# Layer 1 of a five-layer network on Trainium2: modulation by halves, merging products by parts in their own banks, the next norm's transposes taken from X, and GpSimd's bias work later

## The chip, the cores and the metric

The kernel runs on one NeuronCore of one Trainium2 chip. The metric is the device time of one execution in microseconds (us), the median of three runs. "The profile" is that of one further execution; its times count from the first instruction. Engines: PE is TensorE (matrix products), PEld its weight loads, DVE is VectorE, ACT is ScalarE, POOL is GpSimd, SP is SyncE, which issues most transfers here.

## The reference, cut to what matters

Three blocks follow one another on 256 tokens of width 1024; the change touches the first block and the seam to the second.

```python
# block 1
mod = c @ w_ada + b_ada;  shift, scl, gate = split(mod, 3)
h = rms_norm(x, g_norm) * (1 + scl) + shift
u, z_pool, q, k, v, z_attn, m_pool, m_attn = split(h @ w_in, ...)      # 5120 columns
y_pool = (pooling(u) * silu(z_pool)) @ w_pool_up                       # 512 -> 1024
y_attn = (attention(rope(q), rope(k), v) * silu(z_attn)) @ w_attn_up   # 512 -> 1024
merged = sigmoid(m_pool) * y_pool + sigmoid(m_attn) * y_attn
x = x + gate * (merged @ w_out)
x = rms_norm(x, g_final)
# block 2 begins
h = rms_norm(x, ev_attn_norm);  proj = h @ ev_w_in                     # 3072 columns
```

## The kernel before, in words

All weights pass through one stream of chunks of 128x2048 float32 (1 MB), numbered in the order of their use. SP loads chunk n into `ring` (6 slots; it waits until the chunk 6 before it has been split), ACT copies it to `WH` rounded to float32r ("hi", L951), DVE subtracts to give `WL` ("lo", L955); both have 3 slots, so hi of chunk n waits until PE has consumed chunk n-3. PE then makes each product as three: WH with XTH, WL with XTH, WH with XTL (`three`, L400 to L402), where XTH and XTL are the transposed activations, split alike. A full chunk is 24 such instructions. Chunks 0 to 3 are the scale columns of w_ada, 4 to 7 the shift columns, 8 to 27 w_in (`P1`), 28 to 31 the gate columns of w_ada, 32 and 33 w_pool_up (`UP1`), 34 and 35 w_attn_up (`AUP1`), 36 to 39 w_out (`OUT1`), 40 to 51 ev_w_in (`P2`).

The order on every engine is written out by hand, one program per engine; engines meet at semaphores only. `split_until(eng, n)` makes ACT or DVE split all chunks below n at that place of its program, so whatever stands behind it waits for these splits; `used(eng, n)` waits until PE has consumed chunk n. `Transposes` (names beginning with T) lets PE transpose 128x128 tiles (L306) into banks 4 to 7, two tiles per step i; ACT writes XTH (L314), DVE XTL (L327).

Stages in order around the change:

- Modulation (`ada_products`, L2116): the condition vector times w_ada gives rows of 2x512, which are copied to SBUF by `ADA_ROWS` (L1390 on ACT, L1611 on DVE) and turned into columns by tiny products (`ada_columns`, L2125). From these come SCALE and SHIFT (L1616 to L1621), with which ACT makes XTH (L1395) and DVE XT1 and XTL (L1626, L1629) out of the transposed, normed input (`T1`).
- `P1`, heads, pooling and attention `A1`.
- `TY1`, gate products, `TA1`, a product that spreads the gate to all partitions (L2177, banks 6 and 7), `UP1` and `AUP1` into banks 0 to 3, DVE's products with the sigmoids (L1669) after each, one sum (L1672), transposes `TM1`, `OUT1`.
- `OUT1` closes by parts (`PARTS`: half of the columns, tile of tokens): for each part DVE multiplies by the gate (L1685), adds to X (L1686) and multiplies by g_final into O (L1688). `T2` transposes O, `P2` follows. The two norms are merged into one scale per token (`stat`, L1696 to L1702), computed beside P2; POOL then writes the normed X (L1270), which `P2`'s work on DVE waits for at its second job.
- POOL turns the relative-position biases (four transfers issued by ACT at L1420) into the form that a later layer adds (L1264, L1266).

## Time and profile before

| what | value |
|---|---|
| median of 3 runs | 2199.08 us (2198.71 to 2203.82) |
| profiled execution, its own time | 2200.07 us |
| its span, first to last instruction | 2198.3 us |
| PE busy / DVE busy / ACT busy / POOL busy | 92% / 71% / 60% / 5% |
| chain that ended last, by engine | PE 81%, DVE 9%, ACT 6%, issue 3% |
| mean granted TensorE clock | 0.961 of 2.4 GHz |

A clock of 0.5 is 1.2 GHz. Busy shares are means over stages with different limits; the stages in question lie in the first 300 us of the span.

### The profile page before, as it was taken

How to read it: one execution, taken by the hardware profiler on the slowest of the kernel's cores; microseconds unless marked ns; L12 is line 12 of the kernel's file. 1: busy time of each engine (PE TensorE's matmuls, PEld its weight loads, DVE VectorE, ACT ScalarE, POOL GpSimd, SP SyncE). 2: the span in 40 equal slices, each digit the busy share in tenths (PEclk: the TensorE clock that was granted, in tenths of full speed). 3: DMA queues.
4: the chain of work that ended last, by engine and by line, in shares of the span. 5: the costliest groups of instructions: out<-in, count | busy, mean ns of one | idle time of the engine just before them, and what ended most of it. 6: DMA issues, size and time to landing. Idle time of an engine off the chain costs nothing.

```text
span 2198.3 us, 26390 instructions
## 1 busy us (share of the span) xinstructions
PE 2033.0 (92%) x9736; PEld 1674.3 (76%) x9736; DVE 1550.9 (71%) x1719; ACT 1310.8 (60%) x1395; POOL 120.4 (5%) x101
## 2 busy tenths in 40 slices
PE   5998797799999989999999999999999999999687
PEld 2885686678887878787888878787877877787576
DVE  5546673554458678888888888888889854664565
ACT  5445267344444467777777777777776755444243
POOL 0000210000000042000000000000006001000000
PEclk8999899899999999999999999999999999999688
DMA  9554541455545159999999999999999956144100
GB/s 350 170 175 162 155 174 59 154 171 186 195 158 189 58 222 395 364 392 356 389 362 373 384 363 385 358 383 354 391 360 380 348 172 229 53 162 137 39 1 29
DMA packets 233215, 535.16 MB, mean 243 GB/s; under 512 B 12457, under 2 KB 23733, under 8 KB 233142
## 3 DMA queue, kind: packets, MB, share of 16 engines
q1 hardware_dynamic: 222464, 515.80, 65.3%
q10 hardware_dynamic: 8854, 12.07, 1.6%
q0 software_dynamic: 1824, 6.31, 0.8%
q8 instruction: 47, 0.77, 0.1%
q14 instruction: 26, 0.21, 0.0%
HBM read 521.02 MB, written 13.12 MB: 243 GB/s over the span
## 4 chain that ended last, share of the span: by engine, by line
PE 81%; DVE 9%; ACT 6%; issue 3%; DMA 0%; ACTq 0%; DVEq 0%; POOLq 0%; POOL 0%
PE bank L400 23%; PE bank L402 23%; PE bank L401 23%; DVE WL L955 3%; PE bank L514 3%; ACT WH L951 3%; PE bank L526 1%; PE bank L306 1%; PE bank L2341 1%; PE bank L540 1%; PE bank L538 1%; PE bank L536 1%; PE bank L367 1%; ACT XTH L1115 1%; DMA X<-in_x 0%
## 5 line engine op out<-in xcount | busy, mean ns | idle before, releaser
L955 DVE TENSOR_TENSOR WL<-ring,WH 128x2048 fp32r<-128x2048 f32 (+1 forms) x487 | 1118.0, 2308 | 360.4 <-ACT WH L951 358.1
L951 ACT ACTIVATE WH<-ring 128x2048 fp32r<-128x2048 f32 (+1 forms) x487 | 927.8, 1910 | 415.6 <-PE bank L402 404.8
L400 PE MATMUL bank<-WH,XTH 128*128 128x512 f32 (+2 forms) x1936 | 761.0, 393 | 31.0 <-DVE WL L955 7.3
L401 PE MATMUL bank<-WL,XTH 128*128 128x512 f32 (+2 forms) x1936 | 750.6, 388 | 0.0
L402 PE MATMUL bank<-WH,XTL 128*128 128x512 f32 (+2 forms) x1936 | 750.0, 387 | 0.0
L400 PEld LDWEIGHTS bank<-WH,XTH 128*128 128x128 f32 x1936 | 369.6, 191 | 112.3 <-issue 25.1
L402 PEld LDWEIGHTS bank<-WH,XTL 128*128 128x128 f32 x1936 | 369.1, 191 | 74.7
L401 PEld LDWEIGHTS bank<-WL,XTH 128*128 128x128 f32 x1936 | 369.9, 191 | 70.5
L400 PE MATMUL bank<-WH,HTH 128*128 128x512 f32 x540 | 212.7, 394 | 11.3 <-DVE HTL L1915 5.5
L402 PE MATMUL bank<-WH,HTL 128*128 128x512 f32 x540 | 210.2, 389 | 0.0
L401 PE MATMUL bank<-WL,HTH 128*128 128x512 f32 x540 | 209.9, 389 | 0.0
L400 PEld LDWEIGHTS bank<-WH,HTH 128*128 128x128 f32 x540 | 101.4, 188 | 36.5 <-DVE WL L955 14.8
L402 PEld LDWEIGHTS bank<-WH,HTL 128*128 128x128 f32 x540 | 101.5, 188 | 21.3
L401 PEld LDWEIGHTS bank<-WL,HTH 128*128 128x128 f32 x540 | 101.6, 188 | 20.2
L551 ACT ACTIVATE scr<-scr,nmax 128x128 f32<-128x128 f32 (+1 forms) x160 | 71.4, 447 | 71.3 <-DVE nmax L565 71.0
L437 ACT ACTIVATE P<-bank,stat 128x512 f32<-128x512 f32 (+1 forms) x56 | 34.7, 671 | 90.1 <-PE bank L402 90.1
L1529 ACT ACTIVATE P<-bank 128x512 f32<-128x512 f32 x56 | 33.5, 598 | 40.3 <-PE bank L402 40.3
L1333 POOL DMA_INDIRECT P<-rows,P x4 | 6.8, 1701 | 808.4 <-POOLq L1328 807.4
L514 PE MATMUL bank<-KT,QT 128*128 128x256 f32 (+1 forms) x176 | 43.0, 369 | 7.7 <-ACT P L437 2.5
L565 DVE CUSTOM_DVE_ANT_0 scr<-bank,UNSEEN 128x128 f32<-128x128 f32 x96 | 30.4, 355 | 27.2 <-PE bank L514 26.4
L575 DVE COPY scr<-bank 128x384 f32<-128x384 f32 x80 | 44.2, 553 | 3.9 <-PE bank L526 3.9
L1010 ACT ACTIVATE P<-X 128x1024 f32<-128x1024 f32 x14 | 15.1, 1075 | 43.2 <-DVE X L1040 33.7
(405 smaller groups left out, 1553.5 us busy)
## 6 DMA issues: line engine op xcount, KB each, us to landing
ring<-in_od_we_gate SPq DMA_DIRECT2D x112, 1024.0 KB, 6.7
ring<-in_od_we_up SPq DMA_DIRECT2D x112, 1024.0 KB, 7.0
ring<-in_od_we_down SPq DMA_DIRECT2D x112, 1024.0 KB, 6.6
ring<-in_w_in SPq DMA_DIRECT2D x20, 1024.0 KB, 5.2
ring<-in_fox_w_in SPq DMA_DIRECT2D x16, 1024.0 KB, 5.3
ring<-in_nsa_w_in SPq DMA_DIRECT2D x14, 1024.0 KB, 5.0
ring<-in_w_ada SPq DMA_DIRECT2D x12, 1024.0 KB, 8.6
ring<-in_ev_w_in SPq DMA_DIRECT2D x12, 1024.0 KB, 5.1
```

What stands on the lines that cost most here:

```text
L306: last = nc.tensor.transpose(bank[4 + i % 4][:, j * S + tt * 128:j * S + tt * 128 + 128], src(tt), ident[:, :])
L400: nc.tensor.matmul(out, x[0], wt[0][:, k, :], start=start, stop=False, skip_group_check=check)
L401: nc.tensor.matmul(out, x[0], wt[1][:, k, :], start=False, stop=False, skip_group_check=check)
L402: return nc.tensor.matmul(out, x[1], wt[0][:, k, :], start=False, stop=stop, skip_group_check=check)
L437: last = nc.scalar.activation(dest(tt), bank[(2 * c + tt) % 4][:, 0:width], func, scale=stat[:, self.scale + tt:self.scale + tt + 1] if se ...
L514: last = nc.tensor.matmul(b[:, a:a + n], q[:, a:a + 128], k[:, 128 - 128 * t0:256], start=True, stop=not self.pe_mask, skip_group_check=True)
L551: last = nc.scalar.activation(e, e, ACT.Exp, bias=nmax[:, i % 3, t0:t0 + 1], scale=-1.0, accum_out=rs[:, g % 2, t0, uu:uu + 1])
L565: last = nc.vector.tensor_tensor_reduce(out=E[i % 3][:, a:a + n], in0=bank[4 + i % 2][:, a:a + n], in1=self.bias(i, t0), scale=1.0, scalar ...
L575: nc.vector.tensor_copy(PT[j % 2], bank[6 + j % 2][:, 0:384]).then_inc(copied, 1)
L951: nc.scalar.activation(wh, slot_ap(n, nk, width), ACT.Copy).then_inc(hi_made, 1)
L955: nc.vector.tensor_tensor(wl, slot_ap(n, nk, width), wh.bitcast(F32), ALU.subtract).then_inc(lo_made, 1)
L1529: nc.scalar.activation(MHID[:, f % 2, 0, :], bank[f % 2 * 2][:, :], ACT.Silu).then_inc(m_silu, 1)
```

## The change: what it does

1. **Input.** X is loaded by SP ahead of chunk 0, where ACT loaded it beside the ring. The late rows of `vec` (b_ada, g_norm and now g_final) are transposed by PE after chunk 0 in a step of their own; DVE copies them and multiplies g_final by ev_attn there.
2. **Modulation.** The shift columns are read as two halves of 512 columns over all of the depth (chunks 4, 5 and 6, 7), each in its own bank. Each half is turned into columns, and X's columns of that half are made, apart from the other. ACT copies all rows and writes XT1 for even steps. ACT and DVE split chunks 8 and 9 between the halves, where they were split ahead of SHIFT.
3. **Merging.** PE goes from `TA1` straight to `UP1`; `AUP1` writes banks 4 to 7, so it does not wait for DVE. Both close by parts, and DVE multiplies and adds part by part. The spreading of the gate comes after `AUP1`, in banks 0 and 1. `TM1` starts when half of the columns is merged.
4. **Seam.** `T2` transposes X with the scale g_final times ev_attn. DVE's four products with g_final move behind `T2` as two of 128x1024, and the last split of `OUT1` (chunk 41) moves behind these. ACT squares X after `T2`.
5. **POOL** scales X first and works on the biases after it.

```diff
@@ -204,7 +204,8 @@
-        c_scale, c_shift = ada_chunks(1), ada_chunks(0)
+        c_scale = ada_chunks(1)
+        c_shift = [cols(w["w_ada"], 512 * i, 512) for i in range(2)]
@@ -654,18 +656,20 @@
-        UP1 = OutProduct(c_pup, xt)
-        up_used = sem("up_used")
+        up_used, up_ps = sem("up_used"), sem("up_ps")
+        UP1 = OutProduct(c_pup, xt, part_ps=up_ps)
...
-        AUP1 = OutProduct(c_aup, lambda kt, tt: xt(4 + kt, tt))
+        AUP1 = OutProduct(c_aup, lambda kt, tt: xt(4 + kt, tt), lambda half, tt: bank[4 + 2 * half + tt], up_ps)
@@ -708,7 +712,7 @@
-        T2 = Transposes(normed(("ev_attn", 0)), split=True)
+        T2 = Transposes(normed(("g_final", 0), X), split=True)
@@ -1181,6 +1185,8 @@
+            for tt in range(TT):
+                sp.dma_start(X[:, tt, :], t["x"].rearrange("b (t p) n -> p (b t) n", p=128)[:, tt, :]).then_inc(ada_in, 16)
             for n in range(N0):
                 load(n)
@@ -1384,17 +1388,28 @@
-            for i, chunks in enumerate((c_scale, c_shift)):
-                split_until(act, chunks[-1][0] + SPLIT)
-                used(act, chunks[-1][0])
-                nc.scalar.activation(ADA_ROWS[i][:, 0:512], bank[2 * i][0:2, :], ACT.Copy).then_inc(ada_rows, 1)
-            act.wait_ge(ada_set, 2)
-            for i in range(T1.n):
+            split_until(act, c_shift[1][0][0] + 1)
+            used(act, c_scale[-1][0])
+            for h in range(2):
+                nc.scalar.activation(ADA_ROWS[0][:, 512 * h:512 * h + 512], bank[h][0:2, :], ACT.Copy).then_inc(ada_rows, 1)
+            split_until(act, c_shift[1][1][0] + 1)
+
+            def x_columns(i):
                 act.wait_ge(turn_ready, T1.b + i + 1)
-                for k in range(2 * i, 2 * i + 2):
-                    last = nc.scalar.activation(XTH[:, k, :], bank[4 + i][:, k % 2 * S:k % 2 * S + S], ACT.Identity,
-                                                bias=SHIFT[:, k:k + 1], scale=SCALE[:, k:k + 1])
+                for dest in (XTH, XT1) if i % 2 == 0 else (XTH,):
+                    for k in range(2 * i, 2 * i + 2):
+                        out = XTH[:, k, :] if dest is XTH else XT1[:, k // 4, k % 4, :]
+                        last = nc.scalar.activation(out, bank[4 + i][:, k % 2 * S:k % 2 * S + S], ACT.Identity,
+                                                    bias=SHIFT[:, k:k + 1], scale=SCALE[:, k:k + 1])
                 last.then_inc(turn_act, 1)
+
+            for h in range(2):
+                used(act, c_shift[h][-1][0])
+                nc.scalar.activation(ADA_ROWS[1][:, 512 * h:512 * h + 512], bank[2 + h][0:2, :], ACT.Copy).then_inc(ada_rows, 1)
+                act.wait_ge(ada_set, 2 + h)
+                for i in range(2 * h, 2 * h + 2):
+                    x_columns(i)
+                split_until(act, c_in1[0][0][0] + 1 + h)
@@ -1420,13 +1435,11 @@
             OUT1.splits(act)
-            act.wait_ge(x_half, 3)
-            square(act, 0, X)
             T2.act(act)
-            act.wait_ge(x_half, 4)
-            square(act, 1, X)
-            for tt in range(TT):
-                act.wait_ge(y_half, 3 + tt)
+            for tt in range(TT):
+                square(act, tt, X)
+            for tt in range(TT):
+                act.wait_ge(y_half, 1 + tt)
@@ -1655,25 +1669,27 @@
-            split_until(dve, c_gate1[-1][0] + SPLIT)
+            split_until(dve, c_gate1[-1][0] + SPLIT - 1)
+            TA1.dve(dve)
             used(dve, c_gate1[-1][0])
             nc.vector.tensor_copy(GATE_ROWS[0:2, 512:1024], bank[7][0:2, :]).then_inc(gate_rows, 1)
-            TA1.dve(dve)
...
+            for s, (stage, c0) in enumerate(((UP1, 3072), (AUP1, 4096))):
                 stage.splits(dve)
...
+                for i, (half, tt) in enumerate(PARTS):
+                    if i < 3:
+                        dve.wait_ge(up_ps, 3 * s + i + 1)
+                    else:
+                        stage.wait(dve)
+                    m = P[:, tt, c0 + half * 512:c0 + half * 512 + 512]
+                    nc.vector.tensor_tensor(m, stage.outs(half, tt)[:, :], m, ALU.mult).then_inc(up_used, 1)
+                    if s:
+                        dve.wait_ge(up_used, 4 + i + 1)
+                        both_ = P[:, tt, 3072 + half * 512:3584 + half * 512]
+                        nc.vector.tensor_tensor(both_, both_, m, ALU.add).then_inc(merged, 1)
@@ -1684,11 +1700,12 @@
-                dve.wait_ge(x_half, i + 1)
-                nc.vector.tensor_tensor(O[:, tt, at_h], X[:, tt, at_h], GAIN[:, at_h], ALU.mult).then_inc(y_half, 1)
-                if i == 0:
-                    OUT1.splits(dve)
             T2.dve(dve)
+            dve.wait_ge(gfin_in, 16)
+            dve.wait_ge(x_half, 4)
+            for tt in range(TT):
+                nc.vector.tensor_tensor(O[:, tt, :], X[:, tt, :], GAIN, ALU.mult).then_inc(y_half, 1)
+            OUT1.splits(dve)
@@ -2119,21 +2137,26 @@
-            def ada_columns(i):
-                pe.wait_ge(ada_rows, 2 * i + 2)
-                for k in range(KD):
...
+            def ada_columns(row, k0, n, out, count):
+                pe.wait_ge(ada_rows, count)
+                for k in range(n):
...
             ada_products(c_scale[2:], bank[0:2])
-            ada_products(c_shift[0:1], bank[2:4])
-            ada_columns(0)
-            ada_products(c_shift[1:], bank[2:4])
-            ada_columns(1)
+            ada_products(c_shift[0], bank[2:3])
+            ada_columns(0, 0, 8, bank[0], 2)
+            ada_products(c_shift[1][0:1], bank[3:4])
+            ada_columns(1, 0, 4, bank[2], 3)
+            ada_products(c_shift[1][1:], bank[3:4])
+            ada_columns(1, 4, 4, bank[3], 4)
@@ -2172,22 +2195,21 @@
             TA1.pe(pe)
+            UP1.pe(pe, closes=True)
+            TA1.wait(pe)
             pe.wait_ge(gate_rows, 2)
+            AUP1.pe(pe, closes=True)
+            pe.wait_ge(up_used, 4)
             for half_ in range(2):
-                last = nc.tensor.matmul(bank[6 + half_][:, :], ones[0:3, :], GATE_ROWS[0:3, 512 * half_:512 * half_ + 512],
+                last = nc.tensor.matmul(bank[half_][:, :], ones[0:3, :], GATE_ROWS[0:3, 512 * half_:512 * half_ + 512],
                                         start=True, stop=True)
             last.then_inc(gate_ps, 1)
-            UP1.pe(pe)
-            TA1.wait(pe)
-            pe.wait_ge(up_used, 1)
-            AUP1.pe(pe)
-            pe.wait_ge(merged, 1)
+            TM1.pe(pe, lambda i: pe.wait_ge(merged, 2 if i < 2 else 4))
             pe.wait_ge(gate_set, 2)
-            TM1.pe(pe)
             OUT1.pe(pe, operand=TM1, closes=True)
 
 
-            T2.pe(pe, lambda i: pe.wait_ge(y_half, 2 if i < 2 else 4))
+            T2.pe(pe, halves_ready(pe, 0))
```

DVE's queue in the modulation, from the split behind the scale's row on (WL<-ring is a split, the stat rows are SCALE and SHIFT, P<-bank is XT1). Before:

```order
L1618 TENSOR_TENSOR stat<-stat,vec 128x8 [waits dve_chain]
L955 TENSOR_TENSOR WL<-ring,WH 128x2048 [waits hi_made] x4
L1611 COPY P<-bank 2x512 [waits consumed]
L1621 TENSOR_TENSOR stat<-bank,vec 128x8 [waits ada_cols]
L1626 TENSOR_SCALAR P<-bank,stat 128x256 [waits turn_act,ada_set]
```

Of the change:

```order
L1628 TENSOR_TENSOR stat<-stat,vec 128x8 [waits dve_chain]
L959 TENSOR_TENSOR WL<-ring,WH 128x2048 [waits hi_made]
L1632 TENSOR_TENSOR stat<-bank,vec 128x4 [waits ada_cols]
L1642 TENSOR_TENSOR XTL<-P,XTH 128x512 [waits turn_act,ada_set]
L1639 TENSOR_SCALAR P<-bank,stat 128x256 [waits turn_act]
L1639 TENSOR_SCALAR P<-bank,stat 128x256
L1642 TENSOR_TENSOR XTL<-P,XTH 128x512 [waits dve_chain]
L959 TENSOR_TENSOR WL<-ring,WH 128x2048 [waits hi_made]
L1632 TENSOR_TENSOR stat<-bank,vec 128x4 [waits ada_cols]
```

Four splits stood between SCALE and SHIFT; now one does, then half of SHIFT and of X's columns, and the next split follows that.

DVE's queue at the seam, from OUT1's first part on (O<-bank is the gate's product, QT holds the gate, KT g_final, XTL<-bank is T2). Before:

```order
L1685 TENSOR_TENSOR O<-bank,QT 128x512 [waits norm_out_ps,gate_set]
L1686 TENSOR_TENSOR X<-X,O 128x512 [waits dve_chain]
L1688 TENSOR_TENSOR O<-X,KT 128x512 [waits norm_half]
L955 TENSOR_TENSOR WL<-ring,WH 128x2048 [waits hi_made]
L1685 TENSOR_TENSOR O<-bank,QT 128x512 [waits norm_out_ps]
```

Of the change, the last part and what follows it:

```order
L1701 TENSOR_TENSOR O<-bank,QT 128x512 [waits consumed]
L1702 TENSOR_TENSOR X<-X,O 128x512 [waits dve_chain]
L328 SCALAR_TENSOR_TENSOR XTL<-bank,vec,XTH 128x256 [waits turn_act]
...
L1707 TENSOR_TENSOR O<-X,KT 128x1024 [waits norm_half,gfin_in]
L1707 TENSOR_TENSOR O<-X,KT 128x1024
L959 TENSOR_TENSOR WL<-ring,WH 128x2048 [waits hi_made]
```

The split of chunk 41 stood behind the first part and ahead of the other three; it is now the last of all.

POOL's queue around the scaling of X (P<-UNSEEN,P and P<-P are the biases). Before:

```order
L1264 TENSOR_TENSOR P<-UNSEEN,P 128x8x128 [waits rel_in,mask_set]
L1266 TENSOR_SCALAR P<-P 128x8x128
L1264 TENSOR_TENSOR P<-UNSEEN,P 128x8x128
L1266 TENSOR_SCALAR P<-P 128x8x128
L1270 TENSOR_SCALAR X<-O,stat 128x1024 [waits ms_ready,rel_set]
L1270 TENSOR_SCALAR X<-O,stat 128x1024
```

Of the change:

```order
L1269 TENSOR_SCALAR X<-O,stat 128x1024 [waits ms_ready,mask_set]
L1269 TENSOR_SCALAR X<-O,stat 128x1024
L1274 TENSOR_TENSOR P<-UNSEEN,P 128x8x128 [waits rel_in,norm_done]
L1276 TENSOR_SCALAR P<-P 128x8x128
```

The two scalings changed places with the four operations on the biases.

## Rows read from the trace of the kernel before

**Rows 1.** The page: the span.

```profile
span 2198.3 us, 26390 instructions
```

**Rows 2.** The chain that ended last, to P1's first product: start, us, what.

```profile
2.58 10.25 DMA X<-in_x
...
18.45 2.30 DVE WL L955
20.79 3.53 PE bank L2116 x8
...
45.50 3.58 PE bank L2125 x16
...
51.47 0.70 DVE XTL L1629
...
52.31 0.77 PE bank L400
```

**Rows 3.** Timeline of ACT in the modulation: start, us, engine, line, instructions.

```profile
7.88 1.89 ACT L951 ACTIVATE WH<-ring 128x2048 fp32r<-128x2048 f32 x1
...
49.77 3.29 ACT L1395 ACTIVATE XTH<-bank,stat 128x256 fp32r<-128x256 f32 x7
```

**Rows 4.** Windows: chunk 8, UP1, AUP1, OUT1; the number behind POOL is the clock.

```profile
52.30:60.90 8.60, 8.59 (x26) 6.88 (x27) 6.86 (x10) 2.57 (x4) 0.00 (x0) 0.65 0.22 55
203.80:216.70 12.90, 12.82 (x49) 10.06 (x48) 4.63 (x3) 4.80 (x4) 0.00 (x0) 0.87 0.68 219
219.40:233.50 14.10, 14.02 (x48) 10.96 (x48) 4.28 (x3) 1.92 (x1) 0.00 (x0) 0.78 0.29 93
241.60:264.20 22.60, 22.50 (x98) 18.31 (x96) 13.96 (x12) 8.46 (x7) 10.51 (x3) 0.98 0.77 233
```

**Rows 5.** Timeline of PE and DVE from TA1 to TM1.

```profile
198.75 1.04 PE L306 MATMUL bank<-ident,O 128*128 128x128 f32 x8
201.90 1.98 PE L2177 MATMUL bank<-QT,ones 3*128 3x512 f32 x4 [2.11 <-DVE QT L1660]
...
219.40 0.76 PE L400 MATMUL bank<-WH,XTH 128*128 128x512 f32 x1 [2.78 <-DVE P L1669]
...
235.98 2.29 DVE L1672 TENSOR_TENSOR P<-P 128x2048 f32<-128x2048 f32 x1
238.32 3.67 PE L306 MATMUL bank<-ident,P 128*128 128x128 f32 x16 [4.91 <-DVE P L1672]
```

**Rows 6.** Timeline from OUT1 to P2's second job, several engines.

```profile
243.57 4.18 ACTq L1420 DMA_DIRECT2D P<-in_rel  x4
...
262.20 4.47 DVE L955 TENSOR_TENSOR WL<-ring,WH 128x2048 fp32r<-128x2048 f32 x1
...
272.86 1.65 DVE L327 SCALAR_TENSOR_TENSOR XTL<-bank,vec,XTH 128x256 fp32r<-128x256 f32 x4
...
274.62 0.78 PE L400 MATMUL bank<-WH,XTH 128*128 128x512 f32 x1
...
286.77 1.27 ACT L437 ACTIVATE P<-bank,stat 128x512 f32<-128x512 f32 x2 [2.32 <-PE bank L402]
```

**Rows 7.** Timeline of POOL and DVE at the seam.

```profile
253.69 3.21 POOL L1264 TENSOR_TENSOR P<-UNSEEN,P 128x1024 f32<-128x1024 f32 x1 [64.58 <-DMA P<-in_rel]
...
261.68 2.84 POOL L1264 TENSOR_TENSOR P<-UNSEEN,P 128x1024 f32<-128x1024 f32 x1
...
280.64 9.16 POOL L1270 TENSOR_SCALAR X<-O,stat 128x1024 f32<-128x1024 f32 x2 [11.35 <-ACT stat L987]
282.68 4.49 DVE L955 TENSOR_TENSOR WL<-ring,WH 128x2048 fp32r<-128x2048 f32 x2 [2.46 <-ACT WH L951]
288.88 0.95 DVE L1718 TENSOR_SCALAR cs<-cs 128x16 f32<-128x16 f32 x1
...
292.76 4.49 DVE L955 TENSOR_TENSOR WL<-ring,WH 128x2048 fp32r<-128x2048 f32 x2
```

More of the change, by code:

```diff
@@ L1407, in _ @@
             TA1.act(act)
-            act.wait_ge(gate_ps, 1)
-            for half_ in range(2):
-                nc.scalar.activation(GATE[:, 512 * half_:512 * half_ + 512], bank[6 + half_][:, :], ACT.Copy).then_inc(gate_set, 1)
             act.dma_start(GAIN, t["g_final"].partition_broadcast(128)).then_inc(gfin_in, 16)
@@ L1415, in _ @@
             AUP1.splits(act)
+            act.wait_ge(gate_ps, 1)
+            for half_ in range(2):
+                nc.scalar.activation(GATE[:, 512 * half_:512 * half_ + 512], bank[half_][:, :], ACT.Copy).then_inc(gate_set, 1)
             TM1.act(act)
@@ L1595, in _ @@
             dve.wait_ge(vec_ready, 1)
[L1596 removed]
+            link(dve, nc.vector.tensor_copy(vec[:, 0:NVEC_IN], bank[7][:, 0:NVEC_IN]))
             dve.sem_inc(vec_set, 1)
```

93 lines of the change are left out of this document (45 added, 48 removed).

## The prediction

> **What bounds the kernel now.** I read four views, in this order. The page gives the span, 2198.3 us [rows 1]; the execution took 2200.07, so 1.8 us lie around it, and the median of the runs, 2199.08, is 1.0 below the profiled execution. The sum is made against 2200.07. The chain of waits shows where PE is not the limit: in the first 52 us it passes X's transfer, splits, the products of the condition vector and the small column products, and only at 52.31 does PE begin P1's dense products [rows 2]. From there PE is busy almost without a gap to A1, so what starts P1 earlier is kept. The windows then give PE's pace by stage and the granted clock: OUT1 makes 96 products in 22.5 us at clock 0.98, so a chunk of 24 takes about 5.5 us at full clock (2.4 GHz); UP1 and AUP1, 48 products each, take 12.8 and 14.0 at 0.87 and 0.78 instead of 11.0 [rows 4]. The timeline last shows what PE waits for at the merging and at the seam [rows 5, 6]. A chunk's hi costs ACT 1.9 us, its lo DVE 2.25 [rows 3, 7]: against PE's 5.5 these hide in dense stages, unless other work stands ahead of them in their queue.
>
> **The modulation.** Before, X travels 10.25 us and lands at 12.83 [rows 2], while hi of chunk 0 runs at 7.88 [rows 3]. Moved ahead of chunk 0 in SP's queue, X lands some 6.5 us earlier, and chunk 0 about 0.6 us after 7.88. (X is 1 MB; bounds: nothing if the two queues share anyway, 3 us if all of X lies ahead. I take 0.6, since the transfers of both queues were already under way together.) Then hi 8.5 to 10.4, lo to 12.7, PE's eight products at half clock 3.6 (chunk 1's took 3.53 [rows 2]) to 16.3. Behind these comes the new small transpose, and DVE's copy and product wait for it, some 1.0 us, so lo of chunk 1 starts at 17.35 instead of 18.45. The small step thus eats half of what X's arrival gives. Gain here: 1.1.
>
> From there PE's and ACT's steps shift by 1.1 to chunk 5, which PE ends at 33.1. Eight column products (half of the 3.58 [rows 2] at full clock, 2.2 with the gaps) end at 35.3, SCALE follows on DVE, lo of chunk 7 runs 35.8 to 38.1, chunk 6 ends on PE at 38.5, the first half's columns at 39.7, half of SHIFT at 39.9. ACT makes XTH and XT1 for step 0 and XTH for step 1, six operations of 0.47 (seven took 3.29 [rows 3]), to 42.8; then hi of chunk 8 to 44.7, and only then the second half's row, 45.3. Its columns (half clock, 1.8) and lo of chunk 8 both end at 47.1. P1 starts at 47.2 instead of 52.31. Chunk 8 took 8.6 us at clock 0.65 [rows 4]; if so again, it ends at 55.8 instead of 60.9. Chunk 9's hi and lo come behind the second half's columns, at 54.4, just in time. So the gain at chunk 9 is **5.5**: 5.1 by the old clock, up to 6.5 if the clock rises earlier because PE's columns now run straight into P1. Bounds 3 (chunk 0 later by 3, less the slack) and 7.
>
> **The merging.** Before: TA1 ends at 199.8 [rows 5], UP1 starts at 203.8 [rows 4]. PE waits 2.11 for the gate's row and spends 1.98 spreading it. After, UP1 follows TA1, since chunk 32 is split already (of the four splits that ran ahead of the gate's row on DVE it was the third, so it was done some 2.3 ahead of that row): 4.0 gained. UP1 and AUP1 follow PE's dense work without a pause; at full clock they save 1.8 and 3.0. The wait between them, 2.78 [rows 5], goes: 2.8. The lo of chunk 35 still stands ahead of UP1's products on DVE, but they now hold no bank that AUP1 needs.
>
> Behind AUP1: before, products 2.5, the sum 2.3 and transposes to 241.6, 8.2 us from AUP1's end at 233.4. After, lo of chunk 37 ends on DVE 1.2 us before AUP1 does (it starts only when chunk 34 is consumed), and four pairs of product and sum, 0.7 each [rows 2], end at +4.6. TM1's last two steps follow, 8 transposes, 1.0 at full clock [rows 5]: OUT1 starts at +5.8, a gain of 2.4. The spreading product and ACT's copies lie in the wait. Sum for the merging: 4.0 + 1.8 + 3.0 + 2.8 + 2.4 = **14.0**. OUT1 itself: ACT still issues the four bias transfers, 4.18 us [rows 6], ahead of hi of chunk 38; lo of 38 then ends about 10.8 after OUT1's start and PE needs it at 11.0, so it just holds; 0.4 gained if the clock stays full, or lost if it doesn't: 0.4. Bounds for the whole: 11.5 (half clock in one stage, lo of 38 late by 1) and 15.
>
> **The seam.** Before, PE ends OUT1 at 264.1 [rows 4] and P2 starts at 274.62, its second job, chunk 42, at 286.77 [rows 6]: 22.65 after OUT1. The cause is DVE: the lo of chunk 41 took 4.47 instead of 2.25, from 262.20 [rows 6], ahead of three parts. After, the last part is in X at +1.7, T2's last steps take 1.0, P2 starts near +2.8: 7.7 earlier. But that is not what is kept. DVE goes on with T2 (3.4; four of eight took 1.65 [rows 6]) to +5.1, two products of 128x1024 (2.4, by the 2.29 of one of 128x2048 [rows 5]) to +7.5, and only then lo of chunk 41, to +9.9, while PE wants it at +8.3. Chunk 41 runs to +15.4. ACT's hi of 42 waits for the roots, which wait in DVE's queue for that lo: +11.5 to +13.4, lo to +15.7. Chunk 42 starts at +15.7: a gain of 6.9, whatever PE's clock in between.
>
> **POOL.** Its first bias operation took 3.21, the second 2.84 [rows 7]. DVE's split at 262.20 ended 2.15 after POOL's 264.52: it stood still while POOL ran a two-input operation. Against POOL's scaling at 280.64 two splits took 4.49, the plain time, but one small DVE operation took 0.95 and ended as POOL did [rows 7]. In the new order POOL scales from +11.4 to +20.6, then does the biases to about +36, with two-input operations at +20.6 to +23.8 and +28.4 to +31.2 (the others taken as 4.6, like one scaling). DVE there has some twenty small operations (angles, 4.7 us before the split at 292.76 [rows 7]) from +18, then lo of chunk 44, which PE needs at +26.6. Free: done at +25. If the first bias operation also holds the small ones, +27.5, 0.9 late; a second 0.3 comes at chunk 46. I take 1.2; bounds 0 and 4. Seam: 6.9 - 1.2 = **5.7**.
>
> The Trainium skill, SBUF, "Two separate sides", has it that a DVE operation with two SBUF inputs is held for the whole of any GpSimd instruction that reads SBUF, one holder at a time. The split at 262.20 agrees; the two splits under the scaling, at their plain 4.49, do not. By the trace the seam loses 1.2; by this rule of the Trainium skill taken whole, it would lose over 20.
>
> Everything behind P2 keeps its order, and shifts. Sum: 5.5 + 14.0 + 0.4 + 5.7 = 25.6; 2200.07 - 25.6 = 2174.5, against the median about 2173.5. I say **2174**.
>
> **The rivals.**
> 1. Forecast, 2174, its own range 2169 to 2180: 0.66.
> 2. POOL holds DVE more than I take. For it: the small operation held for 0.8. Against it: the two splits unharmed. If each small batch waits for scaling and bias, lo of 44 and 46 are late by 4 in all, with half clock after the waits another 1.5: 2179 to 2182. 0.14.
> 3. The clock and the waits do better: the modulation gives 6.5, merging 15, no hold at the seam and P2's chunk 41 no wait: 2168 to 2170. For it: clocks of 0.65 and 0.78 [rows 4] leave room. 0.11.
> 4. The change does less than it says at the merging: UP1 can't run ahead because splits are late. Where DVE's lo of 33 and 35 stand behind TA1 and the gate's row, UP1 would wait some 2 for each and lose the full clock too; the merging gives 7: 2181. Against it: ACT's hi needs only the chunk three before. 0.05.
> 5. POOL's full hold: POOL's six operations, 9.2 + 3.2 + 2.8 and twice 4.6, or 24.4 us end to end, keep DVE's lo of 42 until +36; chunk 42 starts at +38 instead of +15.7, 22.3 lost (less the 1.2 counted): 2195, no measurable change. Against it stand the two splits at 4.49 under the scaling [rows 7]. 0.02. It is the rule of the Trainium skill, SBUF, "Two separate sides", as worded.
> 6. Slower: the clock. If PE's small column products between chunks leave it at 1.2 GHz when P1 begins, as at 0.65 [rows 4], but for much longer, each chunk of P1 costs 5.5 more; from the fifth chunk the gain of 25.6 is gone, at eight the kernel takes 2218. Against it: chunk 8 shows the clock rising within it. 0.02.
>
> **The numbers.** What a measurement can tell from no change is about 0.3%, 6.6 us, so "same" is 2192.5 to 2205.7. The range 2166 to 2184 takes in cases 1 to 4 but for their tails and leaves out about 0.1. Chances: faster 0.96 (cases 1 to 4), same 0.02, slower 0.02.
>
> **What would show it.** Right: X lands near 6; P1's first product near 47; PE goes from transposes into UP1 near 194 with no wait of 2.78 before AUP1; windows of UP1 and AUP1 at clock 1.00; the first part of P2 within 4 us of OUT1's end, and a wait of 1 to 2 us for lo of chunk 41 in it. Wrong: P1's start above 49 (chunk 0 late, or the small transpose); a lo near 2.3 that lasts 4 to 5 us beside POOL inside P2; PE waits at chunk 44; a clock below 0.9 in OUT1.

## The result and the profile after

The changed kernel takes **2181.33 us** (median of 4 runs, 2180.26 to 2184.28), beside 2198.89 for the kernel before in the same session (4 runs, 2196.35 to 2203.82). The ratio is 0.9924, 95% interval 0.9909 to 0.9939: faster, by 17.6 us of the medians (their quotient is 0.9920). 2174 was forecast, so 7 us of the expected gain are missing. The time lies inside the whole range (2166 to 2184), but outside that of the forecast's own case (2169 to 2180) and inside that of the second rival (2179 to 2182).

The page of the changed kernel; its execution took 2180.26.

```profile
span 2178.5 us, 26399 instructions
```

The span is 19.8 us shorter than that of [rows 1]. The rest follows it from the front. First ACT's timeline at the input, then DVE's (start, us, engine, line, instructions, wait before).

```profile
10.42 1.91 ACT L955 ACTIVATE WH<-ring 128x2048 fp32r<-128x2048 f32 x1 [4.05 <-DMA ring<-in_w_ada]
...
18.32 0.20 DVE L1621 COPY vec<-bank 128x40 f32<-128x40 f32 x1 [0.74 <-PE bank L2149]
...
18.76 6.70 DVE L959 TENSOR_TENSOR WL<-ring,WH 128x2048 fp32r<-128x2048 f32 x3
```

Chunk 0's hi starts at 10.42, where it was 7.88 [rows 3]: with X ahead of it in SP's queue the chunk arrives 2.5 later. X itself is waited for by nobody: ACT and DVE turn to it only behind chunk 0. The lo of chunk 1 starts at 18.76, not at 17.35 as forecast and not even at the old 18.45 [rows 2], behind DVE's copy of the late vector rows, which waited 0.74 for PE's new small transpose (L2149). Yet PE's timeline at P1 has the product where it was expected:

```profile
44.78 1.73 PE L2143 MATMUL bank<-ones,P 2*128 2x1 f32 x8 [3.42 <-ACT P L1408]
46.67 0.80 PE L401 MATMUL bank<-WH,XTH 128*128 128x512 f32 x1 [0.17 <-DVE WL L959]
```

46.67 instead of 52.31. The windows of the changed kernel (the number behind POOL is the granted clock): the first part of P1, UP1, AUP1, OUT1, OUT1's first 4.3 us.

```profile
46.60:55.00 8.40, 8.33 (x26) 6.71 (x27) 6.08 (x8) 6.56 (x9) 0.00 (x0) 0.69 0.78 255
193.70:205.00 11.30, 11.30 (x53) 9.35 (x51) 9.94 (x11) 4.93 (x7) 0.00 (x0) 1.00 1.02 364
206.00:215.80 9.80, 9.80 (x44) 7.85 (x44) 5.87 (x5) 2.78 (x2) 0.00 (x0) 1.00 0.66 221
221.70:245.60 23.90, 23.90 (x100) 19.60 (x99) 12.14 (x13) 8.32 (x7) 0.00 (x0) 0.91 0.74 220
221.70:226.00 4.30, 4.30 (x13) 3.39 (x12) 1.51 (x4) 0.77 (x3) 0.00 (x0) 0.52 0.25 57
```

UP1 and AUP1 run at 2.4 GHz throughout, where they were at 0.87 and 0.78 [rows 4]. OUT1 is the one that lost in this execution: its first 4.3 us are at 0.52, and it takes 24.0 us instead of 22.5. PE's timeline behind AUP1 shows what stands ahead of that:

```profile
215.66 1.98 PE L2204 MATMUL bank<-QT,ones 3*128 3x512 f32 x4
217.57 1.09 PE L307 MATMUL bank<-ident,P 128*128 128x128 f32 x8
220.00 1.97 PE L307 MATMUL bank<-ident,P 128*128 128x128 f32 x8 [1.33 <-DVE P L1689]
221.62 0.78 PE L401 MATMUL bank<-WH,XTH 128*128 128x512 f32 x1
```

OUT1 starts at 221.62 instead of 241.65. Last the seam, in three timelines, of PE, POOL and DVE:

```profile
247.14 1.09 PE L307 MATMUL bank<-ident,X 128*128 128x128 f32 x8 [0.64 <-DVE X L1702]
248.01 0.47 PE L401 MATMUL bank<-WH,XTH 128*128 128x512 f32 x1
...
254.88 0.50 PE L401 MATMUL bank<-WH,XTH 128*128 128x512 f32 x1 [1.15 <-DVE WL L959]
...
277.46 0.77 PE L401 MATMUL bank<-WH,XTH 128*128 128x512 f32 x1 [5.48 <-DVE WL L959]
```

```profile
256.42 9.15 POOL L1269 TENSOR_SCALAR X<-O,stat 128x1024 f32<-128x1024 f32 x2 [73.30 <-ACT stat L991]
265.65 2.43 POOL L1274 TENSOR_TENSOR P<-UNSEEN,P 128x1024 f32<-128x1024 f32 x1
268.06 2.77 POOL L1276 TENSOR_SCALAR P<-P 128x1024 f32<-128x1024 f32 x1
270.80 2.36 POOL L1274 TENSOR_TENSOR P<-UNSEEN,P 128x1024 f32<-128x1024 f32 x1
273.13 2.77 POOL L1276 TENSOR_SCALAR P<-P 128x1024 f32<-128x1024 f32 x1
```

```profile
258.44 4.50 DVE L959 TENSOR_TENSOR WL<-ring,WH 128x2048 fp32r<-128x2048 f32 x2 [2.46 <-ACT WH L955]
262.85 1.00 DVE L1724 CAST stat<-posi 128x2 f32<-128x2 int32 x1
...
264.71 0.89 DVE L1736 TENSOR_SCALAR cs<-cs 128x16 f32<-128x16 f32 x1
...
265.84 2.27 DVE L1738 SCALAR_TENSOR_TENSOR cs<-cs 128x16 f32<-128x16 f32 x1
268.14 0.97 DVE L1739 SCALAR_TENSOR_TENSOR cs<-cs 128x16 f32<-128x16 f32 x1
...
269.78 1.07 DVE L1735 TENSOR_SCALAR cs<-cs 128x16 f32<-128x16 f32 x1
270.89 2.30 DVE L1736 TENSOR_SCALAR cs<-cs 128x16 f32<-128x16 f32 x1
273.22 0.97 DVE L1737 SCALAR_TENSOR_TENSOR cs<-cs 128x16 f32<-128x16 f32 x1
...
275.02 4.49 DVE L959 TENSOR_TENSOR WL<-ring,WH 128x2048 fp32r<-128x2048 f32 x2
```

Read the last two together. Operations on 128x16 elements that take 0.17 by themselves take 2.27 and 2.30, and end (268.11, 273.19) within 0.03 of POOL's two-input operations (268.08, 273.16); L1736 ends at 265.60 and L1735 at 270.85, where POOL's one-input operations do (265.57, 270.83). L1739 and L1737, begun together with POOL's one-input bias operations, take 0.97 and end well before them. The angles take 12.1 us (262.85 to 274.96), where they took 4.7 ahead of the split at 292.76 [rows 7]. The lo of chunk 44 stands behind them, and PE waits 5.48 for it and then runs some three us at half clock.

POOL's first row there holds two operations. In narrower windows of the same timeline they stand apart:

```profile
256.42 2.87 POOL L1269 TENSOR_SCALAR X<-O,stat 128x1024 f32<-128x1024 f32 x1 [73.30 <-ACT stat L991]
259.27 6.29 POOL L1269 TENSOR_SCALAR X<-O,stat 128x1024 f32<-128x1024 f32 x1
```

The second scaling is the same work as the first and lasts 3.4 longer: it stands from 259.27 while DVE's two splits run their plain 4.50 to 262.94, and ends 2.63 behind them. There DVE held POOL. The kernel before has it too: its 9.16 [rows 7] are 2.85 and 6.33.

The stages' gains, from equal instructions of the two traces (before minus after): 6.0 at TY1's transposes (187.80 to 181.80), 20.0 at OUT1's start, 18.5 at OUT1's end (264.10 to 245.62), 26.1 at chunk 42 (ACT's evacuation, 286.77 to 260.67), and 18.5 at the end of P2 (341.26 to 322.78). From there on it moves between 17.4 and 20.6, and is 19.8 at the end.

### The profile page after: what moved, and what is told of

The parts are those of the page before. It is cut to its first block, busy times and chain, and to the rows that moved or that the text cites. A ratio compares the mean times of both kernels' runs of the same rounds, so it can differ in the third digit from the quotient of the medians.

```text
span 2178.5 us, 26399 instructions
## 1 busy us (share of the span) xinstructions
PE 2023.8 (93%) x9737; PEld 1667.7 (77%) x9737; DVE 1551.4 (71%) x1717; ACT 1313.3 (60%) x1401; POOL 106.6 (5%) x101
## 4 chain that ended last, share of the span: by engine, by line
PE 80%; DVE 9%; ACT 7%; issue 3%; DMA 1%; ACTq 0%; DVEq 0%; POOLq 0%; POOL 0%; SPq 0%
PE bank L401 23%; PE bank L403 22%; PE bank L402 22%; DVE WL L959 3%; ACT WH L955 3%; PE bank L516 2%; PE bank L528 1%; PE bank L2363 1%; PE bank L307 1%; PE bank L542 1%; PE bank L540 1%; PE bank L538 1%; PE bank L368 1%; ACT XTH L1119 1%; PE bank L2134 1%
## 5 line engine op out<-in xcount | busy, mean ns | idle before, releaser
L567 DVE CUSTOM_DVE_ANT_0 scr<-bank,UNSEEN 128x128 f32<-128x128 f32 x96 | 30.3, 355 | 25.3 <-PE bank L516 24.4
L528 PE MATMUL bank<-ident,scr 128*128 128x128 f32 x240 | 39.7, 275 | 0.3
```

The lines of the kernel that those rows point to most:

```text
L528: last = nc.tensor.transpose(bank[6 + j % 2][:, c * 128:c * 128 + 128], E[j % 3][:, c * 128:c * 128 + 128], ident[:, :])
L567: last = nc.vector.tensor_tensor_reduce(out=E[i % 3][:, a:a + n], in0=bank[4 + i % 2][:, a:a + n], in1=self.bias(i, t0), scale=1.0, scalar ...
```

## The experiments

Theory of the missing 7 us: POOL's biases, moved behind its scaling, hold DVE's small operations. Rivals: X's place in the queue, the clock in OUT1, and DVE's own queue, which has more work ahead of chunk 44 whatever POOL does. Each kernel is the changed one with the edit shown, unless it says otherwise. The kernel before took 2196.8 to 2197.1 (medians of 11 to 14 runs) beside them, 1.8 to 2.1 less than beside the changed kernel, which was not run again with them; so a difference to its 2181.33 may be off by as much. The ratio's interval is 0.9909 to 0.9939 for the changed kernel. Those of experiments 6, 7, 8 and 11 stand apart from it, that of 5 touches it, and those of all others, 1 and 2 among them, overlap it. Single runs of one kernel spread by 3 to 11 us, so small differences are read from the traces, at the same instruction. Each trace is of one execution, so the part behind OUT1 is best counted from OUT1's end. From there to P2's end (the last evacuation of a bank by ACT) it takes 77.2 in the kernel before and 77.2 in the changed one.

**1. Biases behind the angles.**

```diff
             pool.wait_ge(rel_in, 64)
+            pool.wait_ge(lam_dot, 1)
```

> The changed kernel, with GpSimd's four bias operations held back until the angles on DVE are done. Theory (GpSimd's instructions hold DVE's small operations): the angles, 12.1 us in the changed kernel, fall below 6.5, PE's wait of 5.48 us ahead of chunk 44 goes, and the span ends 5.5 to 7.5 earlier than 2178.5, since the 1.2 GHz stretch behind the wait goes too. Rival (the small operations are slow because X's scaling holds them, or by themselves): less than 2 us. The splits that then lie beside the bias operations may last up to 2.4 longer, twice, hidden by the slack of 2.6 us or more.

Measured: 2177.76 (5 runs), ratio 0.9908 (0.9894 to 0.9921). The profiled span is 5.6 shorter than the changed kernel's, as expected; the median is only 3.6 lower. The timeline of DVE in this kernel:

```profile
264.16 0.89 DVE L1737 TENSOR_SCALAR cs<-cs 128x16 f32<-128x16 f32 x1
...
267.77 6.69 DVE L959 TENSOR_TENSOR WL<-ring,WH 128x2048 fp32r<-128x2048 f32 x2
```

The angles take 5.5 us, with two of them still held by the scaling (1.00 and 0.89), and the wait at chunk 44 is gone. The holds have moved: two splits take 6.69 instead of 4.49 under POOL's next two-input operation, and PE waits 0.94 at chunk 46. From OUT1's end to P2's end it takes 71.1, 6.1 less than in the changed kernel. The gain over the kernel before, read as above, is 25.1 at P2's end; 1.4 of that is an OUT1 that ran 22.6 in this execution instead of 24.0.

**2. The split of chunk 44 ahead of the angles.** POOL is left as it is.

```diff
             def angles():
+                split_until(dve, c_in2[2][0][0] + 1)
```

> The changed kernel, with DVE's split of chunk 44 put ahead of the angles; GpSimd's order stays. Theory: the angles still last about 12 us, chunk 44 is ready when PE wants it, and PE waits for chunk 45 instead, some 2 us (its split then ends near 279.5, wanted at 277.4): the span ends 3 to 5 earlier than 2178.5. Rival (DVE has too much work in this stretch in whatever order): the wait only moves, under 1 us.

Measured: 2177.84 (4 runs), ratio 0.9908 (0.9894 to 0.9923). DVE's timeline:

```profile
264.42 2.29 DVE L959 TENSOR_TENSOR WL<-ring,WH 128x2048 fp32r<-128x2048 f32 x1 [0.91 <-ACT WH L955]
266.63 2.38 DVE L1724 CAST stat<-posi 128x2 f32<-128x2 int32 x1
...
271.80 2.32 DVE L1742 TENSOR_SCALAR cs<-cs 128x16 f32<-128x16 f32 x1
```

The angles are held as before (10.2 us), but only 0.92 of it reaches PE at chunk 45, and 1.40 by way of an evacuation later. From OUT1's end to P2's end it takes 72.8, 4.4 less than in the changed kernel. The profiled span, 2179.1, is not shorter, though 3 to 5 less were expected of it; the median is 3.5 lower. So holding DVE costs nothing by itself; it costs where PE's next split stands behind it.

**3. X back on ACT's queue.**

```diff
             for tt in range(TT):
-                sp.dma_start(X[:, tt, :], ...).then_inc(ada_in, 16)
             for n in range(N0):
                 load(n)
...
             act.dma_start(LATE[32:40, :], ...).then_inc(late_in, 16)
+            for tt in range(TT):
+                act.dma_start(X[:, tt, :], ...).then_inc(ada_in, 16)
```

> The changed kernel, with X loaded from ACT's queue beside the ring again. Theory (X first gives nothing, because chunk 0 then lands 2.5 later): chunk 0 is split from before 8 again, lo of chunk 1 starts within 0.5 of 18.76, P1's first product within 0.5 of 46.67, the time is the same within 1 us. Rival (X's early arrival gives the 1.1 us of the forecast): P1 starts at 47.7 or later and the time is over 1 us longer.

Measured: 2182.03 (6 runs), ratio 0.9926 (0.9913 to 0.9939). Hi of chunk 0 starts at 6.84 again, but X comes so late that the lo of chunk 1 starts at 18.67. PE's timeline at P1:

```profile
47.49 0.79 PE L401 MATMUL bank<-WH,XTH 128*128 128x512 f32 x1 [0.84 <-DVE WL L959]
```

P1 starts 0.82 later than in the changed kernel, outside the 0.5 that was expected. But the same program varies by more: in nine kernels with the changed modulation, one execution each, P1's first product stands between 46.67 and 48.22 (experiment 4). The time is not told from the changed kernel's either. So no effect of X's place on the 6.0 gained in the modulation is shown.

**4. AUP1 in UP1's banks.**

```diff
-        AUP1 = OutProduct(c_aup, ..., lambda half, tt: bank[4 + 2 * half + tt], up_ps)
+        AUP1 = OutProduct(c_aup, ..., part_ps=up_ps)
...
+            pe.wait_ge(up_used, 4)
             AUP1.pe(pe, closes=True)
-            pe.wait_ge(up_used, 4)
```

The gate is spread in banks 6 and 7.

> The changed kernel, with AUP1 writing banks 0 to 3 again, so that it waits for DVE's four products of UP1, and with the gate spread in banks 6 and 7; parts, and the gate after AUP1, stay. Theory (closing by parts had already shortened the wait): PE waits 1.4 to 1.8 us ahead of AUP1, since DVE's last product ends 1.4 after UP1; clock stays near 1.00 in AUP1; the time is 1.4 to 2.5 longer. Rival (the forecast's sum, where the wait of 2.8 and 3.0 of clock belong to the banks): 4 to 6 us longer.

Measured: 2183.51 (4 runs), ratio 0.9937 (0.9923 to 0.9952). PE's timeline:

```profile
206.70 0.47 PE L401 MATMUL bank<-WH,XTH 128*128 128x512 f32 x1 [1.55 <-DVE P L1685]
```

The wait is 1.55 where the kernel before had 2.78 [rows 5]: closing UP1 by parts had already taken 1.2 off it. The clock stays at 1.00 in both stages, so the full clock of AUP1 does not hang on the banks; the rival, which had it so, did not come.

**5. The gate spread ahead of UP1.** The product and ACT's copies stand where they stood before; the banks of the parts stay.

```diff
             TA1.pe(pe)
+            pe.wait_ge(gate_rows, 2)
+            for half_ in range(2):
+                last = nc.tensor.matmul(bank[6 + half_][:, :], ones[0:3, :], ...)
+            last.then_inc(gate_ps, 1)
             UP1.pe(pe, closes=True)
             TA1.wait(pe)
-            pe.wait_ge(gate_rows, 2)
+            pe.wait_ge(gate_set, 2)
             AUP1.pe(pe, closes=True)
-            pe.wait_ge(up_used, 4)
-            for half_ in range(2):
-                last = nc.tensor.matmul(bank[half_][:, :], ones[0:3, :], ...)
-            last.then_inc(gate_ps, 1)
```

> The changed kernel with the gate's row spread by PE ahead of UP1 and copied by ACT ahead of its splits, as before the change; the merging by parts in banks of their own stays. Theory (of the 14.0 gained at the merging 4.0 came from this place, and 1.8 more from UP1's full clock): PE waits about 2 us for the row, takes 2 for the product, UP1 begins at a clock below 0.95, and OUT1 starts 5 to 7 us later: 2186 to 2188. If the copies out of TM1's path make its wait of 1.33 shorter, that gives back up to 0.5. Rival (PE would only reach AUP1's products earlier than DVE's splits allow, so the place doesn't matter): within 1.5 us of the changed kernel, with waits for lo in UP1 and AUP1 in the changed kernel's place.

Measured: 2189.86 (8 runs), ratio 0.9955 (0.9939 to 0.9971), 8.5 above the changed kernel and 1.9 above what was expected. PE's timeline, and the window of UP1:

```profile
197.34 1.98 PE L2200 MATMUL bank<-QT,ones 3*128 3x512 f32 x4 [2.37 <-DVE QT L1675]
199.25 0.50 PE L401 MATMUL bank<-WH,XTH 128*128 128x512 f32 x1
...
228.62 0.78 PE L401 MATMUL bank<-WH,XTH 128*128 128x512 f32 x1
...
199.30:211.50 12.20, 12.20 (x48) 9.87 (x48) 5.30 (x5) 4.80 (x4) 0.00 (x0) 0.86 0.76 227
```

OUT1 starts at 228.62 instead of 221.62. TA1's transposes came 1.1 later by themselves in this execution (192.89 to 193.94, ahead of any edit), so of the 14.0 gained at the merging 5.9 hang on this one place: 2.37 of wait, 1.98 of product and 1.6 of clock in UP1 and AUP1 (199.25 to 222.95 for 96 products, against 22.05 us). From AUP1's end to OUT1 it takes 5.7, against 5.9: two waits of 1.61 and 1.56 stand where the product and one wait of 1.33 stood. The same product behind AUP1 costs next to nothing, because PE waits there for DVE anyway.

**6. POOL's biases ahead of its scaling**, as in the kernel before: the undo of the change's last part.

```diff
-            pool.wait_ge(ms_ready, 2)
-            for tt in range(TT):
-                nc.gpsimd.tensor_scalar(X[:, tt, :], O[:, tt, :], ...)
-            pool.wait_ge(x_done, 2)
             pool.wait_ge(rel_in, 64)
             for j in range(2):
...
+            pool.wait_ge(ms_ready, 2)
+            for tt in range(TT):
+                nc.gpsimd.tensor_scalar(X[:, tt, :], O[:, tt, :], ...)
+            pool.wait_ge(x_done, 2)
```

> The changed kernel with POOL's four bias operations ahead of its X scaling again, as before the change. Theory (POOL's operations hold DVE's wherever they fall): POOL begins them when the rel transfers have landed, near 232, and its first two-input operation falls on DVE's parts and T2's copies or on the lo of chunk 40 or 41; of the 7.6 us lost behind chunk 42 most comes back (the wait of 5.5 at chunk 44 is gone), but X's scaling ends 10 us later, and something near 245 to 255 is held for 2 to 4 us. Net against the changed kernel: 2 to 5 us faster, so near 2177 to 2179, if the scaling isn't needed early. Rival (the late biases are worth what they move): slower than the changed kernel by 2 to 6 us, since OUT1's end and the seam are held as in the kernel before.

Measured: **2174.09** (6 runs, 2172.89 to 2175.45), ratio 0.9887 (0.9869 to 0.9906), better than the best that was expected. POOL's timeline in this kernel, DVE's split beside it, and all that PE still waits for between 245 and 300:

```profile
233.37 3.23 POOL L1270 TENSOR_TENSOR P<-UNSEEN,P 128x1024 f32<-128x1024 f32 x1 [49.95 <-DMA P<-in_rel]
...
242.00 2.77 POOL L1272 TENSOR_SCALAR P<-P 128x1024 f32<-128x1024 f32 x1
...
237.14 2.62 DVE L959 TENSOR_TENSOR WL<-ring,WH 128x2048 fp32r<-128x2048 f32 x1 [2.80 <-ACT WH L955]
...
PE bank L401 <- DVE WL L959: 1.2, 1, 1.2
```

POOL is done at 244.77, 1.2 us before OUT1 ends on PE (245.98). It held one split by 0.33, which nobody waited for. In the kernel before the same four operations lasted to 269.29, 5.2 behind OUT1's end at 264.1, and the lo of chunk 41 took 4.47 [rows 6]. Two of them had taken 4.8 there, where they take 2.8 here. Either began just as a split that POOL had held could run, and ended 2.6 behind that split (261.70 after 259.05, 269.29 after 266.67). The second of them, in the kernel before:

```profile
264.49 4.80 POOL L1266 TENSOR_SCALAR P<-P 128x1024 f32<-128x1024 f32 x1
```

Two things put POOL ahead of the seam here: it begins 12.6 before OUT1's end instead of 10.4, and its four operations take 11.4 instead of 15.6. From OUT1's end to P2's end it takes 70.1, 7.0 less than in the changed kernel.

**7. No biases at all** (P2's attention runs on the rel values as loaded; the four operations are left out).

> The changed kernel without POOL's four bias operations (P2's attention then runs on the unprocessed rel values: this part of the computation is left out). It prices every hold by them. Theory: as in the kernel with the biases behind the angles, no wait of 5.5 at chunk 44, and the lo of chunk 45 or 46 is not held either: 1 to 2 us faster than that kernel, 5 to 7 faster than the changed one, near 2175 to 2176. Rival (the lost 7.6 has another cause as well, DVE's own queue or the clock): less than 4 us faster than the changed kernel, and a wait of over 3 us on DVE between chunks 43 and 46 stays.

Measured: 2171.62 (5 runs, 2171.32 to 2177.61), ratio 0.9876 (0.9855 to 0.9897), 3.4 or more below what was expected. PE waits 1.3 for splits between 245 and 300, nearly all of it the old one at chunk 41 (1.18), and the gain at P2's end is 24.9, with 70.0 from OUT1's end. That is experiment 6's (25.1 and 70.1): up to P2's end, the biases placed there cost nothing. The median is 2.5 lower than experiment 6's, which the intervals do not tell apart.

**8. Experiments 1 and 2 together.**

> The changed kernel with POOL's biases behind DVE's angles and the lo of chunk 44 ahead of the angles. Theory: the two cures act on the same loss, so they don't add: biases later alone left waits of 1.17, 0.16 and 0.94 in P2; with the split ahead the first goes, the one at chunk 46 may stay or grow, because the angles end 2.3 us later and the biases with them. Against the kernel with the biases later 0 to 1.5 us faster: 2176 to 2178. Rival (they add): 2174 or less. Other rival: the biases now fall on the lo of chunk 46 and the heads' sums: 1 to 3 us slower than the biases later alone.

Measured: 2173.58 (6 runs, 2169.85 to 2177.03), ratio 0.9882 (0.9863 to 0.9902). PE waits 1.4 in two places between 245 and 300; the waits of 0.94 and 1.40 are gone. From OUT1's end to P2's end it takes 70.4: 0.8 less than in experiment 1, so the cures add little there. The median is 4.2 below either, where 2176 to 2178 was expected and 2174 or less if they add, but the intervals of the ratios overlap, and the gain at P2's end is 25.1 as in experiment 1. The interval does not separate it from experiment 6 (2174.09) either.

**9. The gain products ahead of T2**, as before.

```diff
-            T2.dve(dve)
             dve.wait_ge(gfin_in, 16)
             dve.wait_ge(x_half, 4)
             for tt in range(TT):
                 nc.vector.tensor_tensor(O[:, tt, :], X[:, tt, :], GAIN, ALU.mult).then_inc(y_half, 1)
+            T2.dve(dve)
             OUT1.splits(dve)
```

> The changed kernel with DVE's two gain products ahead of its part of T2's transposes, as in the kernel before. Theory (the second job of P2, chunk 42, is set by the sum of DVE's work behind OUT1, not by P2's start): P2 starts 2.0 to 2.4 us later, the wait of 1.15 for the lo of chunk 41 goes, and chunk 42's evacuation comes within 0.5 of +15.05 behind OUT1; the time is the changed kernel's within 1 us. Rival (P2's earlier start is kept): chunk 42 and everything behind it come 1.3 to 2.4 later, 2183 to 2185.

Measured: 2181.84 (4 runs), ratio 0.9925 (0.9907 to 0.9943): the time as expected, the way not. PE's timeline:

```profile
249.56 0.47 PE L401 MATMUL bank<-WH,XTH 128*128 128x512 f32 x1 [2.25 <-DVE XTL L328]
...
277.25 0.47 PE L401 MATMUL bank<-WH,XTH 128*128 128x512 f32 x1 [4.06 <-DVE WL L959]
```

and a window of the same kernel, P2's first 5.4 us:

```profile
249.60:255.00 5.40, 5.40 (x17) 4.32 (x18) 5.23 (x14) 4.30 (x7) 0.00 (x0) 0.68 0.00 0
```

OUT1 ended at 244.70 here. P2 starts at +4.9 instead of +2.4 and the wait for chunk 41 is gone, as expected. But behind the longer wait ahead of P2 the clock is at 0.68, and ACT's evacuation at chunk 42 came at +17.65 (262.35), not within 0.5 of +15.05, though DVE had started the lo of chunk 42 at +12.9 as in the changed kernel (+12.8). What is lost so is not kept: at chunk 44 the wait shrinks from 5.48 to 4.06, because there DVE behind POOL sets the pace.

**10. Experiment 6 with the late vector copy behind the lo of chunk 1.**

```diff
+            split_until(dve, c_scale[1][0] + 1)
             dve.wait_ge(vec_ready, 2)
             nc.vector.tensor_copy(vec[:, NVEC_IN:NVEC], ...)
```

> The changed kernel with POOL's biases ahead of its X scaling again, and with DVE's copy of the late vector columns behind the lo of chunk 1 instead of ahead of it. Theory: the lo of chunk 1 starts 0.7 to 1.1 us earlier (17.7 to 18.1 instead of 18.76) and P1 0.5 to 1 earlier; with the 7 us of the biases, 2172 to 2174. Rival: ACT or the transfers set the steps by chunk 3 (P1's first product within 0.3 of 46.67), and the time is that of the kernel with the biases ahead, 2174.

Measured: 2173.76 (5 runs, 2171.20 to 2176.44), ratio 0.9899 (0.9883 to 0.9914). DVE's and PE's timelines:

```profile
17.95 2.29 DVE L959 TENSOR_TENSOR WL<-ring,WH 128x2048 fp32r<-128x2048 f32 x1 [0.38 <-ACT WH L955]
...
46.13 0.80 PE L401 MATMUL bank<-WH,XTH 128*128 128x512 f32 x1 [0.39 <-DVE WL L959]
```

0.81 earlier at chunk 1 and 0.54 at P1, both as expected. They lie just outside what the nine other kernels vary by there (18.76 to 19.35, 46.67 to 48.22), and are too little for the medians.

**11. The last part of the change alone, on the kernel before.** POOL scales first and does the biases after it; all else is before's.

> The kernel before with one part of the change alone: POOL's biases behind its X scaling. Theory (the holds follow the biases; what this part costs is set by where DVE has small operations and splits that PE waits for): the lo of chunk 41 takes 2.25 instead of 4.47, which brings chunk 42 about 2 us earlier, but the angles are held and the lo of chunk 44 comes 5 to 7 us later than now, a wait of 3 to 5.5 for PE; net 1 to 5 us slower than before, ratio 1.001 to 1.002. Rival (the part is good by itself and only the other parts made it harmful): 1 to 2 us faster than before.

Measured: 2202.14 (9 runs), ratio 1.0027 (1.0013 to 1.0041): slower than before. POOL's and PE's timelines, and DVE's split of chunk 41:

```profile
283.97 2.40 POOL L1268 TENSOR_TENSOR P<-UNSEEN,P 128x1024 f32<-128x1024 f32 x1
...
296.39 0.77 PE L400 MATMUL bank<-WH,XTH 128*128 128x512 f32 x1 [3.92 <-DVE WL L955]
...
258.59 2.28 DVE L955 TENSOR_TENSOR WL<-ring,WH 128x2048 fp32r<-128x2048 f32 x1
```

The split of chunk 41 is free (2.28), and P2 starts 8.2 behind OUT1 (260.49 to 268.70) instead of 10.5: 2.3 gained. Counted again from OUT1's end, the first heads' step of P2 (L1743) comes 4.2 later than before: 6.5 lost behind chunk 43. The part is bad by itself too, with a cost at the upper end of what was expected (1 to 5 us; 5.0 by the medians).

## Why the prediction was right, and where 7 us went

**Right in sign and range; one term badly mis-sized.** The forecast's sum was 25.6, and the terms measured add up to 18.5 at P2's end: 6.0 for the modulation, 14.0 for the merging, -1.5 for OUT1, 7.6 for the seam and -7.6 behind it. With POOL's order put back (experiment 6) the trace gains 25.1 there, without the biases 24.9; by the medians it is 22.9 for experiment 6. That the range held is owed to its width, which took in the second rival; of the signs of being wrong that the prediction lists, PE's wait at chunk 44 came, and in part a low clock in OUT1 (0.52 at its start, 0.91 over the stage, where below 0.9 was named).

**The term that was mis-sized** is in the part on POOL: "If the first bias operation also holds the small ones, +27.5, 0.9 late; a second 0.3 comes at chunk 46. I take 1.2; bounds 0 and 4." Measured from chunk 42 to P2's end: 7.6 lost (26.1 less 18.5), of it 5.48 the wait at chunk 44 and 1.5 half clock behind it (eight products in 3.3 us, 1.8 at full clock). In experiment 6 only 0.4 is lost over the same stretch (25.6 at chunk 42, 25.1 at P2's end), so the biases' place cost some 7 of the 7.6. The upper bound of 4 was too low. Most of what it needed was worked out: POOL's operations from +20.6 on (measured +20.0), DVE's angles from +18 (measured +17.2), chunk 44's split behind them, needed at +26.6 (measured +26.4). But only one hold was charged. DVE runs some twenty operations in a row, so each POOL operation that begins while they run takes another one: seven are held, 8.1 us in all (12.1, against 4.0 in experiment 8, where POOL stands still meanwhile). Two of the seven, 1.5 us, belong to the scaling and stay in experiment 1 (5.5); the other five, 6.6 us, are the biases'. The second rival named this with 0.14 and 2179 to 2182, where the time fell; its mechanism is the one that experiments 1, 2, 6 and 7 confirm.

**A reading that was wrong.** The prediction takes each scaling as 4.6, half of the row of 9.16 [rows 7], and the biases' one-input operations like it. The two scalings are 2.85 and 6.33: one takes under 2.9, and the second stood behind DVE's splits. A bias operation of one input took 2.77, so POOL was done at +30.3 and not at +36. Of the two splits under the scaling, the first did run unharmed beside the end of the first scaling (282.68 to 283.49). The second lay beside a scaling that was itself waiting, so it was no sign that POOL's one-input operations do no harm.

The part on POOL was also costed from the wrong side: the prediction compared the new place with nothing, not with where the old order would fall **after the other edits**. Experiment 6 shows that it would have ended ahead of the seam. That undo is worth 7.2 us by the medians, or 5.3 if each kernel is set against the one before in its own session, and 7.0 between OUT1's end and P2's end. But it could not all be foreseen from the rows of before: 4.2 of the 6.4 by which POOL comes earlier there are its shorter operations.

**The Trainium skill**, SBUF — State Buffer, "SBUF: two separate sides", calls the pair of ports that DVE and GpSimd share an exclusive lock, which whichever starts first holds for its whole instruction, while the other blocks. The prediction gives only the half in which GpSimd is first, and so does its fifth rival (2195), which didn't come. This trace agrees for the small operations under POOL's two-input ones (2.27 and 2.30, to the end of POOL's), and the other way round for the second scaling, which lasts 6.29 beside two splits. Under POOL's one-input operations it does not agree in full. The first split, begun at 258.44 under a scaling that ran to 259.28, took its plain 2.29, and in the middle of a bias operation (268.06 to 270.83) three operations of DVE took 0.17 each.

**The modulation**: 5.5 forecast, 6.0 measured, for partly other reasons. X ahead of chunk 0 cost chunk 0 2.5, not 0.6 (inside the bound of 3), so nothing was gained at chunk 1, and experiment 3 shows no effect of X's place. What was gained lies behind it: P1 begins right behind eight column products of 1.73 us, where before sixteen of 3.58 were followed by 3.24 us in which PE waited for X's columns (XTL). Which of the steps of the halves gave how much was not tried apart.

**The merging**: 14.0 forecast and 14.0 measured, at OUT1's start (20.0 less 6.0). Experiment 5 puts 5.9 of it on the gate's place (forecast 4.0 and 1.8 of clock), experiment 4 puts 1.5 on the banks of their own; the rest, some 6.6, lies in the clock of AUP1, the parts and the shorter way to OUT1, which were not tried apart. The term for the wait, 2.8, was thus partly paid by the parts already. That the sum came out to the tenth is luck: one execution differs from the next by more.

**OUT1**: +0.4 forecast, −1.5 measured: ten products at half clock behind the transposes, the "lost if it doesn't" of that step. No split was late. But this is not a fixed price of the change: with the same program up to there and the same wait of 1.33 or 1.32 in the transposes, OUT1 took 22.6 in experiments 1 and 9 and 24.0 to 24.1 in the changed kernel and experiments 2, 7 and 8. What decides between the two is not shown.

**The seam up to chunk 42**: 6.9 forecast; 7.6 measured (26.1 less 18.5). P2 starts 2.4 behind OUT1 (2.8 forecast) and waits 1.15 for chunk 41. The step's addition "whatever PE's clock in between" is wrong: in experiment 9 a later start of P2, its first 5.4 us at 0.68, put chunk 42 2.6 later, with DVE's split at its old place. The size came out near because P2's start and clock (1.00 over chunk 40) stayed ahead of DVE.

## What to carry to other kernels

Work moved on an idle engine is not free if it shares something with a busy one: look for what the busy engine does in that stretch. A long row of short operations ahead of something urgent is a bad neighbour, since each operation of the other engine can hold one or two of them; a large one is held at most once by each, and here it held the other engine as often. When a row of a timeline merges two operations (x2), look at them apart before you take half of it as the time of one. Compare a moved step with where the old order would fall after the other edits, not with where it fell before them. And a small product that PE must make anyway belongs where PE waits for another engine already: the same 2 us of the gate's product cost 5.9 ahead of UP1 and next to nothing behind AUP1.
